# Forward transforms of the long convolutions as three products of parts, and another share-out of the low parts at the seam into block two

## The reference, cut to what matters

```python
h_lat = rms_norm_2(x_lat, g_pre[layer]) * (1 + sc_l[:, None]) + sh_l[:, None]
...
def hyena_mixer(xv, conv_w, conv_b, f_w1, ..., hy_bias):
    x0, x1, v = _split(dw_conv(xv, conv_w, conv_b), (HY_WIDTH, HY_WIDTH, HY_WIDTH))
    filt = hyena_filter(n, f_w1, f_b1, f_freq, f_w2, f_b2, f_w3)
    g = v * x1
    return x0 * (bidir_long_conv(g, filt) + g * hy_bias.astype(g.dtype))

def bidir_long_conv(u, filt):
    n = u.shape[1]
    uf = jnp.fft.rfft(u.astype(jnp.float32), n=2 * n, axis=1)
    ff = jnp.fft.rfft(filt, axis=0)
    return jnp.fft.irfft(uf * ff[None], n=2 * n, axis=1)[:, :n].astype(u.dtype)
```

## Time and profile before

| | us |
|---|---|
| median of three runs | 1667.36 |
| lowest and highest | 1666.48, 1669.48 |
| the profiled execution | 1674.56 |
| its span, first to last instruction | 1672.6 |
| PE busy in the span | 1597.8 |
| DVE busy | 1072.5 |
| ACT busy | 831.1 |

### The profile page before, as it was taken

The page is one execution under the profiler, slowest core; times in us unless marked ns, Lnnn a source line. Parts: engine busy times, 40 slices in busy tenths (PEclk is TensorE's granted clock), DMA queues, the critical chain, the costliest instruction groups (busy, mean ns, idle before and its releaser), DMA issues.

```text
span 1672.6 us, 23419 instructions
## 1 busy us (share of the span) xinstructions
PE 1597.8 (96%) x9108; PEld 1341.7 (80%) x9108; DVE 1072.5 (64%) x1990; ACT 831.1 (50%) x1517; POOL 154.9 (9%) x148
## 2 busy tenths in 40 slices
PE   7988999989989999989999999999999999999998
PEld 7977999878778888867768877787788878787877
DVE  6687777785768778764573656515547855455665
ACT  5855555555656555532303455633336364545564
POOL 0110111210000304100000010100003000000000
PEclk9999999999999999989999999999999999999999
DMA  7536655553355544434401111124522314233333
GB/s 253 175 106 220 218 189 182 183 190 114 115 177 184 181 141 152 163 103 162 164 1 63 51 51 39 57 83 153 178 98 101 114 63 139 81 121 101 101 113 126
DMA packets 61886, 217.70 MB, mean 130 GB/s; under 512 B 7888, under 2 KB 8144, under 8 KB 61648
## 3 DMA queue, kind: packets, MB, share of 16 engines
q1 hardware_dynamic: 58608, 212.40, 37.5%
q10 hardware_dynamic: 3168, 3.80, 0.7%
HBM read 215.09 MB, written 1.05 MB: 129 GB/s over the span
## 4 chain that ended last, share of the span: by engine, by line
PE 66%; DVE 13%; ACT 10%; issue 8%; POOL 2%; ACTq 1%; DMA 0%; DVEq 0%; POOLq 0%
PE PS L344 18%; PE PS L346 17%; PE PS L345 17%; DVE WL L311 3%; ACT WH L294 3%; PE PS L2768 2%; PE PS L2074 2%; PE PS L2083 2%; POOL AR L1590 2%; PE PS L502 1%; PE PS L2148 1%; PE PS L821 1%; PE PS L2125 1%; DVE X L475 1%; PE PS L1927 1%
## 5 line engine op out<-in xcount | busy, mean ns | idle before, releaser
L311 DVE TENSOR_TENSOR WL<-RAWB,WH 128x1024 fp32r<-128x1024 f32 x345 | 425.5, 1238 | 230.8 <-ACT WH L294 225.2
L344 PE MATMUL PS<-RH,WH 128*128 128x256 f32 (+1 forms) x1560 | 505.3, 324 | 15.7 <-DVE WL L311 4.2
L345 PE MATMUL PS<-RH,WH 128*128 128x256 f32 (+1 forms) x1560 | 493.4, 316 | 0.0
L346 PE MATMUL PS<-RH,WL 128*128 128x256 f32 (+1 forms) x1560 | 493.0, 316 | 0.0
L294 ACT CAST WH<-RAWB 128x1024 fp32r<-128x1024 f32 x346 | 358.4, 1041 | 227.1 <-PE PS L346 173.0
L344 PEld LDWEIGHTS PS<-RH,WH 128*128 128x128 f32 x1560 | 300.9, 193 | 50.7 <-issue 13.4
L344 PE MATMUL PS<-WH,RH 128*128 128x512 f32 (+1 forms) x768 | 305.1, 397 | 11.6 <-DVE WL L311 6.7
L346 PEld LDWEIGHTS PS<-RH,WL 128*128 128x128 f32 x1560 | 300.8, 193 | 18.6
L345 PEld LDWEIGHTS PS<-RH,WH 128*128 128x128 f32 x1560 | 301.2, 193 | 18.0 <-issue 0.2
L345 PE MATMUL PS<-WL,RH 128*128 128x512 f32 (+1 forms) x768 | 296.6, 386 | 0.0
L346 PE MATMUL PS<-WH,RH 128*128 128x512 f32 (+1 forms) x768 | 296.4, 386 | 0.0
(11 more groups left out here) (358 smaller groups left out, 1645.9 us busy)
## 6 DMA issues: line engine op xcount, KB each, us to landing
RAWB<-ws SPq DMA_DIRECT2D x394, 512.0 KB, 3.5
TMP<-gains ACTq DMA_DIRECT2D x8, 256.0 KB, 3.1
CS<-cs SPq DMA_DIRECT2D x1, 1472.0 KB, 8.8
X<-x SPq DMA_DIRECT2D x2, 512.0 KB, 3.9
X<-ctx SPq DMA_DIRECT2D x2, 512.0 KB, 8.3
AR<-dec ACTq DMA_DIRECT2D x2, 512.0 KB, 7.1
out<-X SPq DMA_DIRECT2D x4, 256.0 KB, 2.0
AR<-rgw SPq DMA_DIRECT2D x1, 512.0 KB, 5.0
```

The source lines that it names most:

```text
L311: eng.e.tensor_tensor(k.WL[:, i % SPL, :], k.RAWB[:, i % RAW, :], k.WH[:, i % SPL, :].bitcast(F32), ALU.subtract).then_inc(*eng.done("wl", i))
L344: pe.e.matmul(o, wh, xh, start=first, stop=False)
L345: pe.e.matmul(o, wh, xl, start=False, stop=False)
L346: return pe.e.matmul(o, wl, xh, start=False, stop=last)
```

## The change

At the seam into block two, input tiles 0, 4, 1 and 5 (every other one in TURNS) go the way of the last seam: ACT makes the high part from the bank and then shift minus high part, and DVE makes the low part. Tiles 2, 6, 3 and 7 keep the old way with DVE for the shifted tile and ACT for the cast, and POOL now makes the low part of all four. The buffers are halves of two others: `beside` for the shifted tiles and `over` for shift minus high part, two places each. The context tokens, made earlier, are as before.

```diff
+        self.beside = Ring([self.RB[0][:, 256 * i:256 * i + 256] for i in range(2)])
...
+    def whole(self, s, q):
+        return self.beside if (s, q) == ("even2", 0) else self.shifted
... seam_act
         for n, j in enumerate(TURNS):
-            high_act(k, act, m.t, m.q, j, m.high(j), m.gain(j), m.shift and m.shift(j))
+            if m.shift and n % 2 == 0:
+                high_shifted_act(k, act, m.t, m.q, j, m.high(j), m.gain(j), m.shift(j))
+            else:
+                high_act(k, act, m.t, m.q, j, m.high(j), m.gain(j), m.shift and m.shift(j))
... seam_dve
         for n, j in enumerate(TURNS):
-            if m.shift:
+            if m.shift and n % 2:
+                i = TURNS[n - 1]
                 whole_dve(k, dve, m.t, m.q, j, m.gain(j), m.shift(j))
-                if j % 3 != 2:
-                    low_of_whole(k, dve, m.t, m.q, j, m.high(j), m.low(j))
-            else:
+                low_shifted_dve(k, dve, m.t, m.q, i, m.low(i), m.gain(i))
+            elif not m.shift:
                 low_dve(k, dve, m.t, m.q, j, m.high(j), m.low(j), m.gain(j))
... seam_pool
-    for j in TURNS:
-        if m.shift and j % 3 == 2:
-            low_of_whole(k, pool, m.t, m.q, j, m.high(j), m.low(j))
+    for j in TURNS[1::2] if m.shift else ():
+        low_of_whole(k, pool, m.t, m.q, j, m.high(j), m.low(j))
```

```diff
+def turn_unit_act(k, act, L, u):
+    q, c = SPEC_UNITS[(u + 2) % 4]
+    act.wait_ge(*k.PE.at("weights", L.last - 1 + u % 2))
+    if u > 1:
+        act.wait_ge(*k.PE.at("even2", "u", q, c, 1, 1))
+    for tb in range(2):
+        act.wait_ge(*k.PE.at("even2", "gt", u, tb))
+        act.e.activation(L.turned(k, u)[0][:, tb, :], k.ps.of("even2", "gt", u, tb), ACT.Copy)...
+def turn_unit_dve(k, dve, L, u):
+    for tb in range(2):
+        dve.wait_ge(*k.ACT.at("even2", "gt", u, tb))
+        dve.e.tensor_tensor(gl[:, tb, :], k.ps.of("even2", "gt", u, tb), gh[:, tb, :].bitcast(F32), ALU.subtract)...
+        k.ps.free(dve, "even2", "gt", u, tb)
... even2_pe
+        if j == 7:
+            turn_unit_pe(k, pe, L, 0)
         project(k, pe, (s, "cv", j), "e_w_in", 16 + j, rhs, 512, ready)
...
+            pe.wait_ge(*k.DVE.at(s, "table"))
+            pe.wait_ge(*k.DVE.at(s, "gt", u, 1))
-                        mm = pe.e.matmul(b, L.dft(n, 2 * part + fb), g[:, n, :], start=n == 0, stop=n == 1)
+                        mm = three(pe, b, L.forwards(k, n, 2 * part + fb), (gh[:, n, :], gl[:, n, :]), n == 0, n == 1)
... even2_act (the DVE side is the same, with the table's low part)
-        cast_to(k, act, k.ws.chunk(s, "cv", j) + 2)
+        cast_to(k, act, min(k.ws.chunk(s, "cv", j) + 2, L.last))
+        if j == 7:
+            act.wait_ge(*k.PE.at("weights", before(k, L.last + 1)))
+            act_(L.place(k, L.last + 1)[0], k.C("dft"), ACT.Copy).then_inc(*act.done(s, "table"))
+            turn_unit_act(k, act, L, 0)
         conv3_act(k, act, s, "cv", j, L.G[:, j, :], ...)
... after the last turn
+    act.wait_ge(*k.PE.at(s, "u", *SPEC_UNITS[3], 1, 1))
+    cast_to(k, act, L.last + 3)
... even2_dve, after the spectrum of unit 3
+        if (u, p) == (3, 1):
+            rest_to(k, dve, L.last + 3)
```

More of the change, by code:

```diff
@@ L237, in __init__ @@
         self.dv2 = Ring(tmp[0:3])
-        self.rings = [self.over, self.at2, self.dv2, self.ps, self.sq, self.vv, self.junk, self.rb, self.shifted, self.gained,
+        self.rings = [self.beside, self.over, self.at2, self.dv2, self.ps, self.sq, self.vv, self.junk, self.rb, self.shifted, self.gained,
                       *self.modrow]
@@ L517, in high_act @@
         act.wait_ge(*k.DVE.at(s, "shifted", q, j))
-        act.e.activation(hi, k.shifted.of(s, q, j), ACT.Copy).then_inc(*act.done(s, "hh", q, j))
+        act.e.activation(hi, k.whole(s, q).of(s, q, j), ACT.Copy).then_inc(*act.done(s, "hh", q, j))
 def low_dve(k, dve, s, q, j, hi, lo, gain):
@@ L534, in whole_dve @@
     i, c = j // 2, 256 * (j % 2)
-    x = k.shifted.take(dve, s, q, j)
+    x = k.whole(s, q).take(dve, s, q, j)
     dve.wait_ge(*k.PE.at(s, "turned", q, i, 1))
@@ L545, in low_of_whole @@
     eng.wait_ge(*k.ACT.at(s, "hh", q, j))
-    eng.e.tensor_tensor(lo, k.shifted.of(s, q, j), hi.bitcast(F32), ALU.subtract).then_inc(*eng.done(s, "hl", q, j))
-    k.shifted.free(eng, s, q, j)
+    eng.e.tensor_tensor(lo, k.whole(s, q).of(s, q, j), hi.bitcast(F32), ALU.subtract).then_inc(*eng.done(s, "hl", q, j))
+    k.whole(s, q).free(eng, s, q, j)
 def high_shifted_act(k, act, s, q, j, hi, gain, shift):
@@ L1861, in __init__, with place, turned, forwards @@
         self.HH, self.Y = k.rview(0, 8, 512), k.rview(8192, 8, 512)
-        self.dft = lambda n, f: k.C("dft")[:, 512 * n + 128 * f:512 * n + 128 * f + 128]
+        self.last = k.ws.chunk("even2", "cv", 7)
         self.XT = k.ring("e2xt", [k.C("dft")[:, 256 * i:256 * i + 256] for i in range(2)])
         self.idft = lambda f: k.C("idft")[:, 256 * f:256 * f + 256]
+    def place(self, k, n):
+        return k.WH[:, n % SPL, :], k.WL[:, n % SPL, :]
+    def turned(self, k, u):
+        return [t.rearrange("p (a b) -> p a b", a=2) for t in self.place(k, self.last - 1 + u % 2)]
+    def forwards(self, k, n, f):
+        return [t[:, 512 * n + 128 * f:512 * n + 128 * f + 128] for t in self.place(k, self.last + 1)]
     def mags(self, c, n):
@@ L2036, in split_dve, with turn_unit_pe @@
     dve.e.tensor_tensor(lo, src, hi.bitcast(F32), ALU.subtract).then_inc(*dve.done(s, kind, j, "yl"))
+def turn_unit_pe(k, pe, L, u):
+    q, c = SPEC_UNITS[u]
+    for tb in range(2):
+        b = k.ps.take(pe, "even2", "gt", u, tb)
+        c0 = 256 * q + 128 * tb
+        for jj in range(4):
+            pe.wait_ge(*k.DVE.at("even2", "g", 4 * c + jj))
+            t = pe.e.transpose(b[:, 128 * jj:128 * jj + 128], L.G[:, 4 * c + jj, c0:c0 + 128], k.ident)
+        t.then_inc(*pe.done("even2", "gt", u, tb))
+def turn_unit_act(k, act, L, u):
[5 more added lines that the diff above has]
+        act.wait_ge(*k.PE.at("even2", "gt", u, tb))
+        act.e.activation(L.turned(k, u)[0][:, tb, :], k.ps.of("even2", "gt", u, tb), ACT.Copy).then_inc(
+            *act.done("even2", "gt", u, tb))
+def turn_unit_dve(k, dve, L, u):
+    gh, gl = L.turned(k, u)
+    for tb in range(2):
+        dve.wait_ge(*k.ACT.at("even2", "gt", u, tb))
+        dve.e.tensor_tensor(gl[:, tb, :], k.ps.of("even2", "gt", u, tb), gh[:, tb, :].bitcast(F32), ALU.subtract).then_inc(
+            *dve.done("even2", "gt", u, tb))
+        k.ps.free(dve, "even2", "gt", u, tb)
 def even2_pe(k, pe):
@@ L2041, in even2_pe @@
     seam_pe(k, pe, seams(k)[s])
-    ready = normed_ready(k, s, (0, 1), lambda k, q, i: k.POOL if q == 1 or i % 3 == 2 else k.DVE)
+    ready = normed_ready(k, s, (0, 1), lambda k, q, i: k.POOL if q == 1 or i in TURNS[1::2] else k.DVE)
     rhs = operand(L.HH)
@@ L2056, in even2_pe @@
             k.ps.drop("mod", SEAM_GROUP[s] if j == 0 else 7)
-    for q, c, p in SPEC_STEPS:
+    for u, p in SPEC_STEPS:
+        q, c = SPEC_UNITS[u]
         if p == 0:
[L2059 to L2065, removed]
+            turn_unit_pe(k, pe, L, u)
         elif p == 1:
-            for tb in range(2):
-                pe.wait_ge(*k.ACT.at(s, "gt", q, c, tb))
-            g = L.GT.of(s, q, c)
+            pe.wait_ge(*k.DVE.at(s, "table"))
+            pe.wait_ge(*k.DVE.at(s, "gt", u, 1))
+            gh, gl = L.turned(k, u)
             for fb in range(2):
@@ L2210, in even2_act @@
     for j in range(8):
-        cast_to(k, act, k.ws.chunk(s, "x1", j) + 2)
+        cast_to(k, act, min(k.ws.chunk(s, "x1", j) + 2, L.last))
         x = k.sq.take(act, s, "x1", j)
         conv3_act(k, act, s, "x1", j, x, k.P("ecw", 24 + 8 + j), k.P("ecb", 8 + j))
-        cast_to(k, act, k.ws.chunk(s, "cv", j) + 2)
+        cast_to(k, act, min(k.ws.chunk(s, "cv", j) + 2, L.last))
[3 more added lines that the diff above has]
+            turn_unit_act(k, act, L, 0)
         conv3_act(k, act, s, "cv", j, L.G[:, j, :], k.P("ecw", 24 + 16 + j), k.P("ecb", 16 + j))
-    for q, c, p in SPEC_STEPS:
+    for u, p in SPEC_STEPS:
         if p == 0:
[L2218 to L2222, removed]
+            turn_unit_act(k, act, L, u)
+    act.wait_ge(*k.PE.at(s, "u", *SPEC_UNITS[3], 1, 1))
+    cast_to(k, act, L.last + 3)
     act.mark(s, "convolved")
@@ L2363, in even2_dve @@
             mod_turn_dve(k, dve, 7)
-        rest_to(k, dve, k.ws.chunk(s, "cv", j) + 2)
+        rest_to(k, dve, min(k.ws.chunk(s, "cv", j) + 2, L.last))
+        if j == 7:
+            hi, lo = L.place(k, L.last + 1)
+            dve.wait_ge(*k.ACT.at(s, "table"))
+            v.tensor_tensor(lo, k.C("dft"), hi.bitcast(F32), ALU.subtract).then_inc(*dve.done(s, "table"))
+            turn_unit_dve(k, dve, L, 0)
         conv3_dve(k, dve, s, "cv", j, L.G[:, j, :], k.P("ecw", 16 + j), k.P("ecw", 48 + 16 + j))
```

16 lines of the change are left out of this document (9 added, 7 removed).

## The result

The changed kernel takes 1659.0 us as a median of five runs (1657.3 to 1661.6), the kernel before 1667.4; the ratio is 0.995 with a 95% interval of 0.9935 to 0.9964, that is 6.0 to 10.8 us less. Two later samples gave 0.9937 (0.9915 to 0.996) and 0.9935 (0.9915 to 0.9954). Over all 17 runs of it and 70 of the kernel before (the five beside this sample and 65 later ones) the means are 1659.9 and 1670.6: 10.7 us. I had predicted 12.3 us and 1655.0. The time lies in the range, 4 us above the point.

What follows compares the result with a forecast made beforehand. PE, busy 96% of the span, was taken as the bound. Transforms 6.0 plus seam 6.3 made 12.3 us, so 1667.4 would become 1655.0 us; the range was 1651 to 1660.5.

Steps and rivals of the forecast that it cites:

- What bounds the kernel: Whole kernel: PE, busy 96% of the span, bounds it; time won at the seam arrives unshortened at the transforms.
- The transforms, PE: Forward steps: three fp32r matmuls at 0.227 us replace each float32 product of 0.859, a gain of 5.7 us.
- the three products stand in the open: Rival, 3%: in the transforms the fp32r matmuls do not hide their weight loads, 0.42 us each; kernel at 1673.6.
- The transforms, holes, DVE and the late chunks: Around `cv` 7, 0.3 us gained; DVE follows, 11.0 of 13.2 us per unit (rival 9%, 1657.5); late chunk splits cost nothing.
- The seam, the pace: Seam into block two: input tiles come at 0.75 us each, `x1` 0 ends at 731.2 instead of 736.1, 4.9 us.
- The seam, the clock: Behind the seam: with a hole of only 1.0 us the clock holds, so L833 and six matmuls gain 1.4 us more.
- The difference between profile and median: Whole kernel: the median's 7.2 us below the profiled execution is taken over unchanged, as not sitting in these stages.
- The spread between runs: Whole kernel: two runs differ by 0.2% or 3.3 us at most, also the limit for telling no change.
- The clock falls again at the seam: Rival, 20%: at the seam the clock drops despite the shorter hole, costing about 3 us, 1658.0.
- The gain is given back behind: Rival, 4%: the attention's first projections wait for late raw loads or ACT's queue, some 8 us back, 1663.

## Why the prediction was right, and the term that was too large

**What bounds the kernel: right.** No wait of PE between the seam and the transforms, and what each half won arrived at the end: 3.5 + 6.5 against 9.3 us at equal clock. The plain medians are too blunt to show it.

**The transforms, PE: right.** A forward step of 24 matmuls takes 5.48 us, a pitch of 0.228 us with both operands in the weight slots where I had taken 0.227; "the three products stand in the open" is out.

**The transforms, holes, DVE and the late chunks: right.** 0.4 us of slack before backwards 0 where I had 0.2; the turn ahead of `cv` 7 is worth 2.7 us if taken away; with one product less DVE binds at once. As a rival it had no turn here, but it is the next bound.

**The seam, the pace: right against one trace.** "That is 4.9 us": 4.8 there. But part of the old seam's 15.0 us was itself run at the low clock; with the clock up it is 13.75 against 9.73, 4.0 us.

**The seam, the clock: the term that was mis-sized.** I took the fall at 732 from the one trace as what the kernel before always does, and added 1.4 us for its end. Two other traces of the old seam have no such fall. Against these two my sum of 6.3 would be 3.8 (15.66, their mean, less 11.88, the mean of the three new ones), and with the fall counted once in three traces 4.6.

**The difference between profile and median: wrong.** "Nothing suggests that the difference sits in these stages, so I take it over." The profiled execution had a clock of 0.987 and lay 7.2 us above the median shown; 2.6 us of that were in the seam I was pricing (18.3 against 15.7). A gain worked out against the falls of one such execution does not carry over to the median. With 4.6 for the seam the sum would have been 4.6 + 6.1 = 10.7 us; the first sample had 8.3, all runs 10.7 (1.2 either way).

**The spread between runs: wrong, and the base with it.** "Two runs of this kernel differ by 0.2% or 3.3 us at most" came from three runs. The 70 runs of it spread over 12 us, and the median of the 65 later ones is 1670.5, 3.2 us above the 1667.4 from which I subtracted; whether the draw or the chip made the first sample low is not known. From 1670.5 the same sum would have given 1658.2, where the median of the 17 runs of the changed kernel is 1660.0. So the larger part of the 4 us by which the time lies above my point is the base, not the gain. Between the later runs' gain by the means (10.9) and at equal clock (9.3) lie 1.6 us that go with the changed kernel's higher mean clock. Whether the new seam brings that, having no fall at 732 to lose, or only the draw, is not shown.

**The rivals.** "The clock falls again at the seam": it did not fall behind the holes of 0.69 to 1.17 in any trace of the new seam. "The gain is given back behind": no wait of PE in the attention changed (3.9, 3.3 and 0.7 us before and after).

## What to carry to other kernels

A single trace is one draw: before a clock fall in it goes into the sum, ask whether the medians carry it, by the distance between the profiled time and the runs and by the mean clock of each. Three runs are a small sample too, when the kernel spreads over 12 us. Where PE stands still for 3 us at a seam, work of any kind in that hole can be worth having: four such holes filled were worth 3.4 to 4.4 us here, and the filler, which ended before the awaited operand, did not hold up what follows. When products are made cheaper, count the work of the engine that reads them from its first instruction on: here 7.3 us less for PE brought 2.1 us by the end of the transforms, because PE then waited for DVE and the wait also brought the clock down.

## What the runs showed of the hardware

At one and the same hole of 2.99 to 3.07 us ahead of the second turns the granted clock fell in some executions and not in others. In the ten traces that have it, the clock fell to 1.2 GHz, in the hole or behind it, every time at the first two seams, in five at the third and in six at the last, mostly for a short stretch and in three cases for one about twice as long. Filled up to 0.99 to 1.06 us it never fell there (eight seams in two traces); at 2.00 to 2.07 it fell at two of three.

The length of a hole alone does not decide it. In the attention of the first trace of before the clock fell behind holes of 1.09 and 0.75 us, while it stayed up behind the same two (1.08 and 0.75, at 988.64 and 990.52) in the changed kernel's trace:

```profile
1001.89 1.93 PE L2148 MATMUL PS<-AR 128*128 128x128 f32 x8 [0.75 <-ACT AR L2279]
```
```profile
1002.00:1003.00 1.00, 1.00 (x6) 0.54 0.00 0
```

The 70 runs of the kernel before spread from 1666.4 to 1678.3 us, those with a clock on record from 0.994 to 0.985, and a microsecond of lost clock costs 0.71 us of time in the fit. The low part L546 on DVE beside POOL's, 0.60 instead of 0.42 us, has no successor in the new seam: the four L573 that took its place have 0.48 each, though two of them (724.05 and 730.22) run into POOL's low parts by 0.1 us. That L546 ended at 725.73, 0.27 us behind POOL's, sooner than if it had waited for the whole of it, as far as POOL's rough times can tell.
